# Branch B of a hybrid attention block: the low parts of the next head pair's tiles move from GpSimd to VectorE, and the transposed probabilities' low part moves ahead of a normalisation

## The reference, cut to what matters

```python
qb = rms_norm(b_cq, q_a_norm_w) @ w_q_b            # (512, 8 * (128 + 64))
kvb = rms_norm(b_ckv, kv_a_norm_w) @ w_kv_b        # (512, 8 * (128 + 128))
qb_rope, kb_rope = apply_rope(...), apply_rope(b_kr)   # 64 wide, key shared by the heads
s = (q_nope . k_nope + q_rope . k_rope) * (128 + 64) ** -0.5
s = where(k_chunk <= q_chunk, s, -1e30)            # block-causal, chunks of 64
out_b = softmax(s) @ v * silu(b_g)                 # per 128-query block and head
```

## Time and profile before

| what | value |
|---|---|
| time, median of 3 runs | 733.1 us (732.21 to 733.49) |
| span of the profiled execution, first to last instruction | 731.0 us |
| median less that span | 2.1 us |
| mixer B with the pairs pipelined | about 445 to 570 us of the span |
| busy share of TensorE matmul / weight load / VectorE / ScalarE / GpSimd | 96 / 80 / 51 / 42 / 44 % |

### The profile page before, as it was taken

One profiled execution on the slowest core, in us unless ns is written; L12 is line 12 of the kernel. 1 busy time (PEld: TensorE's weight loads), 2 busy tenths in 40 slices (PEclk: granted clock), 3 DMA queues, 4 the chain that ended last, 5 costly groups with the idle time before them and its releaser, 6 DMA issues.

```text
span 731.0 us, 10045 instructions
## 1 busy us (share of the span) xinstructions
PE 704.1 (96%) x3482; PEld 586.1 (80%) x3482; DVE 371.9 (51%) x678; ACT 305.7 (42%) x605; POOL 323.6 (44%) x150
## 2 busy tenths in 40 slices
PE   5999999999989999999999998999999999999995
PEld 4888887888868888888888887787778888888884
DVE  6958022990995476475575576767753110100113
ACT  7722131212144363464464476665655132312333
POOL 3554433444353333233244226454566366474630
PEclk9999999999999999999999999999999999999999
DMA  8642232223222122112212213102101843232215
GB/s 287 208 142 87 88 114 87 87 89 113 86 67 78 59 86 86 57 62 92 76 48 95 86 58 116 59 30 87 58 30 58 312 160 104 86 101 100 87 40 219
DMA packets 21293, 72.84 MB, mean 100 GB/s; under 512 B 2320, under 2 KB 2448, under 8 KB 21136
## 3 DMA queue, kind: packets, MB, share of 16 engines
q1 hardware_dynamic: 18144, 66.07, 26.9%
q10 hardware_dynamic: 3120, 6.38, 2.4%
HBM read 68.24 MB, written 4.19 MB: 99 GB/s over the span
## 4 chain that ended last, share of the span: by engine, by line
PE 65%; issue 12%; DVE 9%; POOL 9%; ACT 3%; DMA 1%; POOLq 0%; DVEq 0%; ACTq 0%; SPq 0%
PE bank L895 19%; PE bank L899 19%; PE bank L898 19%; POOL w_lo L235 7%; POOL y L298 2%; DVE t L596 2%; DVE t L755 2%; PE bank L993 1%; PE bank L980 1%; PE bank L1098 1%; DVE pb L794 1%; PE bank L979 1%; DVE st_b L786 1%; PE bank L996 1%; POOL mx_lo L255 1%
## 5 line engine op out<-in xcount | busy, mean ns | idle before, releaser
L235 POOL TENSOR_TENSOR w_lo<-w_raw,w_hi 128x1024 fp32r<-128x1024 f32 x109 | 268.3, 2465 | 341.6 <-ACT w_hi L308 340.9
L308 ACT ACTIVATE w_hi<-w_raw 128x1024 fp32r<-128x1024 f32 x110 | 115.8, 1057 | 252.7 <-PE bank L895 221.1
L895 PE MATMUL bank<-x_hi,w_hi 128*128 128x512 f32 x520 | 208.7, 401 | 2.9 <-DVE t L596 2.9
L899 PE MATMUL bank<-x_lo,w_hi 128*128 128x512 f32 x520 | 203.6, 392 | 0.0
L898 PE MATMUL bank<-x_hi,w_lo 128*128 128x512 f32 x520 | 203.2, 391 | 0.0
L895 PEld LDWEIGHTS bank<-x_hi,w_hi 128*128 128x128 f32 x520 | 98.3, 189 | 22.5 <-DVE t L596 3.3
L899 PEld LDWEIGHTS bank<-x_lo,w_hi 128*128 128x128 f32 x520 | 98.0, 188 | 21.1
L898 PEld LDWEIGHTS bank<-x_hi,w_lo 128*128 128x128 f32 x520 | 98.2, 189 | 19.4 <-issue 0.5
L895 PE MATMUL bank<-w_hi,mx_hi 128*128 128x512 f32 x256 | 101.0, 394 | 0.1
L899 PE MATMUL bank<-w_lo,mx_hi 128*128 128x512 f32 x256 | 99.9, 390 | 0.0
L898 PE MATMUL bank<-w_hi,mx_lo 128*128 128x512 f32 x256 | 99.9, 390 | 0.0
(11 more groups left out here) (190 smaller groups left out, 1043.8 us busy)
## 6 DMA issues: line engine op xcount, KB each, us to landing
w_raw<-w_stream SPq DMA_DIRECT2D x110, 512.0 KB, 3.3
xs<-x_t SPq DMA_DIRECT2D x8, 512.0 KB, 4.3
y<-x_nat ACTq DMA_DIRECT2D x4, 1024.0 KB, 8.5
out<-y SPq DMA_DIRECT2D x8, 512.0 KB, 3.1
fw<-final_w ACTq DMA_DIRECT2D x1, 1024.0 KB, 16.7
cos_r<-tables ACTq DMA_DIRECT2D x1, 256.0 KB, 3.7
sin_r<-tables ACTq DMA_DIRECT2D x1, 256.0 KB, 4.2
cos_b<-tables ACTq DMA_DIRECT2D x1, 256.0 KB, 2.8
```

What stands on the lines that cost most here:

```text
L235: pool.tensor_tensor(w_lo[:, s % HL, :], w_raw[:, s % RAW, :], w_hi[:, s % HL, :].bitcast(F32), ALU.subtract)\
L308: act.activation(w_hi[:, s % HL, :], w_raw[:, s % RAW, :], ACT.Copy).then_inc(w_hi_ready, 1)
L895: ins = pe.matmul(dst, ah, bh, start=start, stop=False)
L899: return pe.matmul(dst, ah, bl, start=False, stop=stop)
```

## The change

It has two parts. First, GpSimd's `b_tile_low` and ScalarE's copy into `b_tmp` go; VectorE's `b_tile_low` now serves all pairs, reading the bank, in the same filler slots: in a filler it stands behind the rotary's operations and ahead of the normalisation that is still late. TensorE's `bank_free` waits for `b_lo` in every pair. Second, at a T step VectorE issues the low part of the transposed probabilities first and the late normalisation after it, in place of the other way round; this is so in all four pairs.

```diff
--- before.py
+++ after.py
@@ -100,8 +100,6 @@
         ptb_hi = at("ptb_hi", [P, TOK, SEQ], F32R, r_x + 48 * KB)
         ptb_lo = at("ptb_lo", [P, TOK, SEQ], F32R, r_x + 56 * KB)
 
-
-        b_tmp = at("b_tmp", [P, 2, SEQ], F32, r_x + 28 * KB)
 
         r_mixed = region(MIX_TILES * SEQ * 4)
 
@@ -235,19 +233,6 @@
                 pool.tensor_tensor(w_lo[:, s % HL, :], w_raw[:, s % RAW, :], w_hi[:, s % HL, :].bitcast(F32), ALU.subtract)\
                     .then_inc(w_lo_ready, 1)
 
-            def b_tile_low(p, j):
-
-                n, par = 6 * p + SPLIT[j], p % 2
-                pool.wait_ge(b_hi, n + 1)
-                src = b_tmp[:, n % 2, :]
-                if j in (1, 2):
-                    dst, hi = vb_lo[par][:, 2 * j - 2:2 * j, :], vb_hi[par][:, 2 * j - 2:2 * j, :]
-                    src = src.rearrange("p (a b) -> p a b", a=2)
-                else:
-                    dst, hi = (kn_lo, kn_hi) if j in (0, 3) else (qn_lo, qn_hi)
-                    dst, hi = dst[par][:, j in (3, 6), :], hi[par][:, j in (3, 6), :]
-                pool.tensor_tensor(dst, src, hi.bitcast(F32), ALU.subtract).then_inc(b_lo, 1)
-
             def mixed_low(j):
                 pool.wait_ge(m_hi, j + 1)
                 if j == 6:
@@ -268,8 +253,6 @@
             for p in range(PAIRS):
                 for f in range(len(B_PIECES)):
                     if p < PAIRS - 1:
-                        if f in B_SPLITS:
-                            b_tile_low(p + 1, B_SPLITS[f])
                         if f in B_CHUNKS:
                             c = PB0 + 3 * (p + 1) + B_CHUNKS[f] + AHEAD
                             low_part(c, c)
@@ -421,13 +404,10 @@
 
             def b_tile_high(p, j):
 
-                idx, n = PB_TILES * p + j, 6 * p + SPLIT[j]
+                idx = PB_TILES * p + j
                 par, bk = p % 2, B[idx % 4]
                 scale = B_SCALE if j >= 5 else 1.0
                 act.wait_ge(proj_done, T_PB + idx + 1)
-                if p > 0:
-                    act.wait_ge(b_lo, n - 1)
-                    act.activation(b_tmp[:, n % 2, :], bk[:, :], ACT.Copy, scale=scale)
                 if j in (1, 2):
                     dst, src = vb_hi[par][:, 2 * j - 2:2 * j, :], bk[:, :].rearrange("p (a b) -> p a b", a=2)
                 else:
@@ -758,12 +738,12 @@
                     dve.wait_ge(b_rot_evac, p + 1)
                     dve.tensor_tensor(t3[:, :], t1[:, :], t2[:, :], ALU.add).then_inc(b_rot, 1)
 
-            def b_tile_low(j):
-
-                par, bk = 0, B[j % 4]
-                dve.wait_ge(b_hi, SPLIT[j] + 1)
+            def b_tile_low(p, j):
+
+                par, bk = p % 2, B[(PB_TILES * p + j) % 4]
+                dve.wait_ge(b_hi, 6 * p + SPLIT[j] + 1)
                 if j >= 5:
-                    hi, lo = qn_hi[0][:, j - 5, :], qn_lo[0][:, j - 5, :]
+                    hi, lo = qn_hi[par][:, j - 5, :], qn_lo[par][:, j - 5, :]
                     dve.scalar_tensor_tensor(out=lo, in0=bk[:, :], scalar=B_SCALE, op0=ALU.mult, in1=hi.bitcast(F32), op1=ALU.subtract)\
                         .then_inc(b_lo, 1)
                     return
@@ -804,12 +784,12 @@
                 m = mixed[:, A_TILES + head, :]
                 dve.tensor_tensor(m, B[7][:, :], m, ALU.mult).then_inc(b_out, 1)
 
-            b_tile_low(0)
+            b_tile_low(0, 0)
             for k in range(CQ_T):
                 dve.wait_ge(cqs_split, k + 1)
                 dve.tensor_tensor(cqs_lo[:, k, :], cq[:, k, :], cqs_hi[:, k, :].bitcast(F32), ALU.subtract).then_inc(lat_lo, 1)
             for j in (1, 2, 3):
-                b_tile_low(j)
+                b_tile_low(0, j)
 
             dve.wait_ge(rot_landed, 32)
             dve.tensor_scalar(cos_b[:, :], cos_b[:, :], B_SCALE, None, ALU.mult)
@@ -817,9 +797,9 @@
             dve.wait_ge(consts_set, 8)
             for part in range(2):
                 b_rotary(0, part)
-            b_tile_low(5)
+            b_tile_low(0, 5)
             b_rotary_low(0)
-            b_tile_low(6)
+            b_tile_low(0, 6)
             dve.wait_ge(gate_silu, 16)
             for p in range(PAIRS):
                 f, late = 0, None
@@ -832,9 +812,6 @@
                         late = w
                         continue
                     if step[0] == "T":
-                        if late is not None:
-                            b_normalise(late)
-                            late = None
                         b_pt_low(w)
                     elif step == "V0":
                         continue
@@ -848,6 +825,8 @@
                                 b_rotary(p + 1, B_ROTARY[f])
                             if f == 8:
                                 b_rotary_low(p + 1)
+                            if f in B_SPLITS:
+                                b_tile_low(p + 1, B_SPLITS[f])
                         if f == 9:
                             b_take(2 * p)
                         f += 1
@@ -1042,10 +1021,8 @@
                 p, j = divmod(idx - 4, PB_TILES)
                 if j == 4:
                     pe.wait_ge(b_rot_evac, p + 1)
-                elif p == 0:
-                    pe.wait_ge(b_lo, SPLIT[j] + 1)
                 else:
-                    pe.wait_ge(b_hi, 6 * p + SPLIT[j] + 1)
+                    pe.wait_ge(b_lo, 6 * p + SPLIT[j] + 1)
 
             def b_project(p, j, ks):
 
```

## The result

The changed kernel took 737.6 us (median of 6 executions, 735.25 to 738.2), the kernel before, beside it, 734.0 us (median of 6). The ratio is 1.0043 with a 95% interval of 1.0027 to 1.0059; of 734.0 us that is +3.2 us, between +2.0 and +4.3: slower, as forecast. The predicted 736.5 was 733.1 + 3.4.

What follows compares the result with a forecast made beforehand. TensorE bounds the kernel, so only its waits, nearly all at the transposes, move the time. Terms -0.2 + 1.8 + 1.5 + 1.5 - 1.1 = +3.5 us, taken as 3.4: 733.1 + 3.4 = 736.5, range 733.6 to 738.6.

Steps and rivals of the forecast that it cites:

- T2, pairs 0 to 2: Transposition of unit 2 in each pair: 0.1 us later in pair 0, 0.17 earlier in pairs 1 and 2; sum -0.2.
- T3, pairs 0 to 2 (tile 2): Transposition of unit 3: a new wait of 0.6 us in three pairs, from tile 2's subtraction; +1.8.
- T6, pairs 0 to 2 (tile 3): Transposition of unit 6: waits 0.5 us more, three times, from tile 3's subtraction and the later transposition of unit 3; +1.5.
- T7, pairs 0 to 2 (tile 5): Transposition of unit 7: waits 0.5 us more, three times, tile 5's subtraction standing ahead of unit 6's low part; +1.5.
- pair 3, T2 and T3: Pair without subtractions: the new order saves 0.4 us at unit 2's transposition and 0.7 at unit 3's; -1.1.
- hand-over T7 to next T0: From a pair's last transposition to the next pair's first: tile 6's subtraction delays a maximum 0.6 us, but hidden; nothing.
- The swap: Low part before late normalisation at T steps: alone saves 1.0 us in pairs 0 to 2, 1.1 in pair 3; 2.1.
- The chain of tile 2: VectorE's low part of unit 1, scaling of unit 3, subtraction, then maximum of unit 4 at 456.74, not 455.69.
- Costed at nothing: Removed ScalarE copies and GpSimd subtractions, tile 6, tile 0 of pairs 1 and 2, the moved `bank_free` wait: no time.
- Relief pays: Rival: without GpSimd's subtractions VectorE's scalings are no longer held, covering the new work; only 2.1 us saved, 731.0; chance 0.10.
- Half of it: Rival: chain behind unit 3's transposition recovers, unit 6's only 0.1 later; +1.4, so 734.5 us; chance 0.13.
- a second wait: Rival: rotary's sum in filler 7 shifts into GpSimd's chunks and is held, at most twice; 738.4 us; chance 0.05.

Runs made afterwards that it cites:

- e1: The kernel before with only the new order at the T steps, GpSimd keeping the low parts: 0.9974 of before.
- e5: The changed kernel with tile 2's subtraction moved behind the maximum of unit 4: 1.0012 of before.
- e8: The changed kernel with tile 3's subtraction alone moved behind the maximum of unit 5: 1.0031 of before.
- e6: The changed kernel with tile 5's subtraction moved behind the low part of unit 6: 1.0019 of before.
- e4: The changed kernel plus a 512-wide GpSimd subtraction for each of the 18 tiles, into scratch that nobody reads: 1.0171 of before.
- e9: e1 with the five rotary products one filler earlier, ahead of the maximum of unit 6: 1.0085 of before.
- e3: The changed kernel with subtractions of tiles 0 to 3 behind the next maximum, tile 5's behind the low part of unit 6: 0.9973 of before.
- e7: e3 with the low part of unit 5 also ahead of the scaling of unit 7: 0.9981 of before.

## Why the prediction was right

Term by term, prediction against the intervals of the changed kernel less those of before:

| term | predicted, us | measured, us |
|---|---|---|
| T2, pairs 0 to 2 | -0.2 (+0.1, -0.17, -0.17) | -0.45 (+0.02, -0.22, -0.25) |
| T3, pairs 0 to 2 (tile 2) | +1.8 | +1.63 |
| T6, pairs 0 to 2 (tile 3) | +1.5 | +1.27 |
| T7, pairs 0 to 2 (tile 5) | +1.5 | +1.57 |
| pair 3, T2 and T3 | -1.1 | -1.15 |
| hand-over T7 to next T0 | 0 | -0.25 |

The measured terms add up to 2.6; the rest to 2.7 is spread over the other intervals. The forecast of +3.4 was 0.7 too high by this. T2, T6 and the hand-over were each 0.2 to 0.3 too high, T3 0.2. That +3.4 lies nearer to the +3.2 of the measured ratio is luck, within its interval of 2.0 to 4.3. The 736.5 lies 1.1 below the measured 737.6 mostly because the kernel before came out at 734.0 and not 733.1 this time.

- *What bounds it.* TensorE, and its waits at the transposes: right. Both kernels' TensorE work is equal. (The wait at T3 of pair 3, for which the prediction names rows 3, is the row at 548.32 above; rows 3 are of pair 0.)
- *The swap.* 0.32 us at T2, from one pair of rows, and 1.1 us in pair 3: e1 gave 0.32 three times and 1.14. Right.
- *The chain of tile 2.* VectorE's timeline of the changed kernel, around it:

```profile
455.10 0.42 DVE L779 TENSOR_TENSOR ptb_lo<-bank,ptb_hi 128x256 fp32r<-128x256 f32 x1 [1.18 <-ACT ptb_hi L430]
...
455.63 0.49 DVE L774 TENSOR_SCALAR pb<-pb,st_b 128x512 f32<-128x512 f32 x1
...
456.03 0.68 DVE L754 TENSOR_TENSOR vb_lo<-bank,vb_hi 128x512 fp32r<-128x512 f32 x1
...
456.63 0.28 DVE L766 TENSOR_REDUCE st_b<-bank 128x1 f32<-128x128 f32 x1
...
457.87 0.56 DVE L779 TENSOR_TENSOR ptb_lo<-bank,ptb_hi 128x384 fp32r<-128x384 f32 x1 [0.96 <-ACT ptb_hi L430]
```

The order and the distances are those of the working: low part, scaling, subtraction back to back, the maximum of unit 4 1.53 us behind the start of the low part (worked out: 456.74 - 455.18 = 1.56). The subtraction takes 0.68 and holds the next by 0.60. Right; e5 undoes it.
- *Tile 3 and T6.* The size was 0.43 each and not 0.5. The text has both T3's lateness and tile 3's place in this term; e5 and e8 show that tile 3's place alone carries it.
- *Tile 5 and T7.* 0.5, measured 0.52; e6 undoes it.
- *Costed at nothing.* Tile 6, tile 0 of pairs 1 and 2, ScalarE's copies and the wait of `bank_free`. The first two are right: T0 to T1 grows by 0.04 us at most. TensorE shows no wait at a bank in the changed kernel. What ScalarE's copies alone are worth no run shows. The hand-over gave back 0.08 us per pair. The prediction had said that nobody on TensorE waited for GpSimd's subtractions, and that was wrong here: in the kernel before, the next pair's first scores waited for GpSimd's low part of tile 5. This row of the kernel before ends at 472.02, and the scores began at 472.17:

```profile
470.65 1.37 POOL L249 TENSOR_TENSOR qn_lo<-b_tmp,qn_hi 128x512 fp32r<-128x512 f32 x1 [4.62 <-ACT qn_hi L435]
```

- *The rivals.* "Relief pays" did not come about at the place that decides, for the reason given (no scaling was held there). But the reason was read from the kernel before, where GpSimd's subtractions lay elsewhere against VectorE's; e4 shows that in the new order a subtraction on GpSimd holds them right there. Taking GpSimd's work away was a condition for the small loss, and I had costed it at nothing: this was not foreseen, and the sum came out right without it because the scaling of unit 3 was priced unheld. "Half of it" and "a second wait" did not occur; the latter's mechanism, a sum held by a chunk, is what sank e9.

No version here is shown to beat the swap alone: e1, e3 and e7 are at 0.9974, 0.9973 and 0.9981 of before, and their intervals overlap. All three are faster than both kernels.

## What to carry to other kernels

Before work moves to an engine with idle time, ask what it will stand ahead of: 15 of the 18 subtractions cost 4.7 us more ahead of the maxima and the low parts that TensorE waits for than behind them, where they cost 0.2 (e3 less e1). Reordering for a shorter chain and adding work to the same engine must be worked out together, along one timeline: here the one alone gave -2.2, the other +1.5, and the two +2.7 us. Where a chain has room for one delay, the second is the one that is paid. And a hold of VectorE beside GpSimd, read as harmless in one order of the work, has to be read again in the new one.

## What I had not expected of the hardware

A VectorE instruction that was ready in the same hundredth of a microsecond as GpSimd's (both at 456.28 in e4) was the one that waited, for 0.8 us, and 18 such GpSimd operations of 1.0 to 1.2 us, whose results nobody reads, made mixer B longer by 9.3 us, 1.6 of them through the clock. Nor had the clock been looked for: the same 1.95 us of idle TensorE was followed by a fall to the lower level in six of the profiles and not in the other six. In e9 one late maximum held VectorE itself 1.3 us later, through ScalarE's queue and GpSimd.
